# Moving the shared expert's down products and the overflow tables of a mixture-of-experts stage from the first pair of units to a place behind the seventh pair

## What is computed

```python
N_EXPERTS = 64
TOP_K = 8
D_EXPERT = 256
def moe(h, lp):
...
    def block(args):
        tb, gb = args
        a = jax.nn.silu(jnp.einsum('td,edf->tef', tb, lp['w_exp_gate'])) * jnp.einsum('td,edf->tef', tb, lp['w_exp_up'])
        a = a * gb[:, :, None].astype(a.dtype)
        return jnp.einsum('tef,efd->td', a, lp['w_exp_down'])
...
    shared = (jax.nn.silu(t @ lp['w_sh_gate']) * (t @ lp['w_sh_up'])) @ lp['w_sh_down']
    return (routed + shared).reshape(b_, l_, d)
```

## Time and profile before

| | |
|---|---|
| median of 3 runs | 787.26 us |
| the profiled execution | 786.93 us |
| its span | 785.1 us |
| PE busy | 742.6 us (95%) |
| DVE, ACT, POOL busy | 383.4, 136.3, 42.9 us |
| moved by DMA | 268.72 MB, mean 342 GB/s |
| time outside the span | 1.83 us |

### The profile page before, as it was taken

The page is one execution under the profiler, slowest core; times in us unless marked ns, Lnnn a source line. Parts: engine busy times, 40 slices in busy tenths (PEclk is TensorE's granted clock), DMA queues, the critical chain, the costliest instruction groups (busy, mean ns, idle before and its releaser), DMA issues.

```text
span 785.1 us, 13758 instructions
## 1 busy us (share of the span) xinstructions
PE 742.6 (95%) x5059; PEld 357.3 (46%) x5059; DVE 383.4 (49%) x869; ACT 136.3 (17%) x290; POOL 42.9 (5%) x49
## 2 busy tenths in 40 slices
PE   4999999889999999999999999899999999999988
PEld 0554434566555454544444444344444443444433
DVE  2236368483786334454454354344543454435456
ACT  3124001410111121111111111111110111111110
POOL 0000001000000110110100101101001011010100
PEclk9999999999999999999999999999999999999999
DMA  9993465650818969999999999999999999999992
GB/s 342 386 386 141 172 237 233 243 175 21 312 33 349 355 241 383 399 420 419 418 419 421 418 422 418 418 421 418 421 419 419 421 417 421 419 419 421 419 389 84
DMA packets 52218, 268.72 MB, mean 342 GB/s; under 512 B 6556, under 2 KB 8988, under 8 KB 27104
## 3 DMA queue, kind: packets, MB, share of 16 engines
q1 hardware_dynamic: 47584, 255.78, 81.0%
q0 software_dynamic: 4608, 12.59, 4.2%
HBM read 269.01 MB, written 3.52 MB: 347 GB/s over the span
## 4 chain that ended last, share of the span: by engine, by line
PE 59%; DMA 31%; DVE 5%; SPq 2%; issue 2%; ACT 1%; DVEq 0%; ACTq 0%
PE ps L555 55%; DMA raw_gu<-in_w_exp_up 29%; PE ps L1011 1%; DMA ada<-in_w_ada 1%; SPq L484 1%; SPq L485 0%; PE ps L866 0%; DVE probT L1624 0%; DVE x L1698 0%; PE ps L1038 0%; DVE xtmp L1696 0%; PE ps L632 0%; DVE h L1722 0%; DVE keyT L1569 0%; DVE h L1723 0%
## 5 line engine op out<-in xcount | busy, mean ns | idle before, releaser
L555 PE MATMUL ps<-raw_gu,xs 128*32 128x512 f32 x2048 | 226.1, 593 | 18.1 <-DMA raw_gu<-in_w_exp_up 16.7
L555 PEld LDWEIGHTS ps<-raw_gu,xs 128*32 128x32 f32 x2048 | 68.9, 110 | 172.5 <-issue 157.6
L555 PE MATMUL ps<-raw_dn,ast 128*32 128x512 f32 x824 | 116.3, 595 | 0.1
L1971 DVE TENSOR_TENSOR acc<-acc,ps 128x512 f32<-128x512 f32 x180 | 109.9, 678 | 0.0
L1928 DVE SCALAR_TENSOR_TENSOR act_a<-ps,small,sil 128x256 f32<-128x256 f32 x32 | 15.5, 484 | 192.1 <-ACT sil L1334 192.1
L555 PE MATMUL ps<-ys,place 128*128 128x512 f32 x360 | 98.4, 409 | 0.0
L555 PEld LDWEIGHTS ps<-ys,place 128*128 128x128 f32 x360 | 63.3, 189 | 35.7 <-issue 25.1
L1964 DVE TENSOR_TENSOR ys<-ps,ys 128x512 fp32r<-128x512 f32 x60 | 41.5, 691 | 66.0 <-ACT ys L1347 66.0
L555 PEld LDWEIGHTS ps<-raw_dn,ast 128*32 128x32 f32 x824 | 28.8, 109 | 60.4 <-issue 58.2
L1347 ACT CAST ys<-ps 128x512 fp32r<-128x512 f32 x60 | 35.1, 585 | 111.7 <-PE ps L555 111.7
L2080 POOL DMA_INDIRECT xg<-h_spill,slot_row x30 | 29.7, 988 | 435.5 <-DVE slot_row L1882 430.9
(11 more groups left out here) (319 smaller groups left out, 692.3 us busy)
## 6 DMA issues: line engine op xcount, KB each, us to landing
raw_gu<-in_w_exp_gate SPq DMA_DIRECT2D x64, 1024.0 KB, 16.0
raw_gu<-in_w_exp_up SPq DMA_DIRECT2D x64, 1024.0 KB, 18.1
raw_dn<-in_w_exp_down SPq DMA_DIRECT2D x48, 1024.0 KB, 16.8
ada<-in_w_ada SPq DMA_DIRECT2D x16, 512.0 KB, 11.3
ada2a<-in_w_ada SPq DMA_DIRECT2D x8, 1024.0 KB, 4.6
ada2b<-in_w_ada SPq DMA_DIRECT2D x8, 1024.0 KB, 6.2
raw_dn11a<-in_w_exp_down SPq DMA_DIRECT2D x16, 512.0 KB, 17.3
raw_dn11b<-in_w_exp_down SPq DMA_DIRECT2D x16, 512.0 KB, 21.1
```

Of the source, the lines that this page charges most:

```text
L555: return nc.tensor.matmul(out, l, r, start=first, stop=last)
L1971: V.tensor_tensor(a, a, ps[:, 4 + (6 * half + k) % 4, :], ALU.add).then_inc(S["acc_done"], 1)
```

## The change

The three `shared_down` and `over_tables` leave pair 0 on PE and stand behind the loop over pairs 1 to 6, in PSUM banks of their own numbering (`rest`, banks 4 to 7), between `down(6, 1)` and `up(7, 0)`. `shared_turn` stays. ACT's six copies into `acc` go; DVE starts `acc` by copying the first scattered results instead of adding them, and behind pair 6 it makes the tables and adds the six shared results to `acc`. PE starts pair 7 when all nine results are taken. SP, ACT, DVE and POOL get a second loop each, so that the first (up to pair 6) needs no table; the read of `jobs` and the wait for `tables_ready` stand between the two. `sh_aT` moves to other addresses. The core of the diff:

```diff
+        rest = ["overR", "overJ", "overK"] + [f"sd{t}{n}" for t in range(NT) for n in range(2)]
+        SPLIT = WIDE // 2 + 1
+        def rbank(n):
+            return ps[:, 4 + rest_no[n] % 4, :]
...
-            sp.wait_ge(S["tables_ready"], 1)
-            n_pairs = sp.value_load(jobs[0:1, NJOB:NJOB + 1], min_val=NMAIN // 2, max_val=NUNIT // 2)
-            with sp.Fori(1, n_pairs - 1) as p:
+            with sp.Fori(1, SPLIT) as p:
+                next_weights(p)
+            sp.wait_ge(S["tables_ready"], 1)
+            n_pairs = sp.value_load(jobs[0:1, NJOB:NJOB + 1], min_val=NMAIN // 2, max_val=NUNIT // 2)
+            with sp.Fori(SPLIT, n_pairs - 1) as p:
+                next_weights(p)
...
+            def open_rest(n):
+                if rest_no[n] > 3:
+                    pe.wait_ge(S["rest_taken"], rest_no[n] - 3)
+                return rbank(n)
...
             shared_turn(2)
-            pe.wait_ge(S["hr_sb"], hr_no["sa2"] + 1)
-            shared_down(0)
             turn(0, 0, True)
-            over_tables()
-            shared_down(1)
             pe.wait_ge(S["misc_sb"], freed_all)
             pe.wait_ge(xg_in[1], 16)
             for n in range(2):
                 tokens_t(1, n)
-            shared_down(2)
             pe.wait_ge(S["pick_ready"], 2)
             pe.wait_ge(S["ast_ready"], 2)
             gate_slots(2)
             pe.wait_ge(S["hr_sb"], len(hr))
             down(0, 0, False)
...
-            with pe.Fori(1, WIDE // 2 + 1) as p:
+            with pe.Fori(1, SPLIT) as p:
                 pair(p, True)
-            with pe.Fori(WIDE // 2 + 1, final) as p:
+            pe.wait_ge(S["xs_act"], 2 * SPLIT + 2)
+            pe.wait_ge(S["xs_dve"], 2 * SPLIT + 2)
+            over_tables()
+            for t in range(NT):
+                shared_down(t)
+            pe.wait_ge(S["tables_ready"], 1)
+            n_pairs = pe.value_load(jobs[0:1, NJOB:NJOB + 1], min_val=NMAIN // 2, max_val=NUNIT // 2)
+            final = pe.value_load(jobs[0:1, NJOB + 1:NJOB + 2], min_val=NMAIN // 2 - 1, max_val=NUNIT // 2 - 1)
+            pe.wait_ge(S["rest_taken"], len(rest))
+            with pe.Fori(SPLIT, final) as p:
                 pair(p, False)
...
-            shared_out(0)
             take_turned(0, 0)
-            shared_out(1)
             tokens(0, 1)
-            shared_out(2)
...
-            add_scattered(0, 1)
+            for k in range(6):
+                dve.wait_ge(S["scat_done"], 6 + k + 1)
+                V.tensor_copy(acc[:, k // 2, k % 2 * 512:(k % 2 + 1) * 512], ps[:, 4 + (6 + k) % 4, :]).then_inc(S["acc_done"], 1)
...
+            with dve.Fori(1, SPLIT) as p:
+                pair(p)
+            i = take_rest("overR")
...
+            dve.sem_inc(S["tables_ready"], 1)
+            dve.wait_ge(S["acc_done"], 12 * SPLIT)
+            for t in range(NT):
+                for n in range(2):
+                    a = acc[:, t, n * 512:(n + 1) * 512]
+                    taken(V.tensor_tensor(a, a, take_rest(f"sd{t}{n}"), ALU.add))
...
+            with pool.Fori(0, SPLIT) as p:
+                pool.wait_ge(S["xt_done"], 4 * p + 4)
+                gather(p + 1)
             pool.wait_ge(S["tables_ready"], 1)
```

More of the change, by code:

```diff
@@ L270, in build @@
         sh_a = [at(f"sh_a{t}", 58 + t, [P, DE]) for t in range(NT)]
-        sh_aT = [at(f"sh_aT{t}", 74 + t, [P, 2, P]) for t in range(NT)]
+        sh_aT = [at(f"sh_aT{t}", (201, 202, 123)[t], [P, 2, P]) for t in range(NT)]
         acc = at("acc", 34, [P, NT, D])
@@ L363, in build @@
                 + ["A20", "A21", "pv2", "mT10", "mT11", "o2", "mT20", "mT21"]
-                + ["pos", "key", "tabR", "tabP", "tabG", "tabJ", "tabK", "start", "overR", "overJ", "overK"])
+                + ["pos", "key", "tabR", "tabP", "tabG", "tabJ", "tabK", "start"])
         misc_no = {n: k for k, n in enumerate(misc)}
@@ L377, in build @@
         hr = [f"{n}{t}{x}" for t in range(NT) for n, x in (("h", 0), ("h", 1), ("r", ""))] \
-            + [f"sa{t}" for t in range(NT)] + [f"sd{t}{n}" for t in range(NT) for n in range(2)]
+            + [f"sa{t}" for t in range(NT)]
         hr_no = {n: k for k, n in enumerate(hr)}
@@ L391, in hbank @@
         def hbank(n, w=512):
-            if n[0:2] == "sd":
-                return ps[:, 1 + int(n[3]), 0:w]
             return ps[:, hr_no[n] % 2, 0:w]
         combos = [(0, 0), (1, 0), (0, 1), (1, 2)]
+        rest = ["overR", "overJ", "overK"] + [f"sd{t}{n}" for t in range(NT) for n in range(2)]
+        rest_no = {n: k for k, n in enumerate(rest)}
+        SPLIT = WIDE // 2 + 1
+        def rbank(n):
+            return ps[:, 4 + rest_no[n] % 4, :]
         last_order = [(n, t) for n in range(2) for t in (1, 2, 0)]
@@ L999, in over_tables @@
                     last = mm(w, ones[0:NE], offs[0:NE].unsqueeze(2).to_broadcast([NE, NOVER, 2]), False, True)
-                last.then_inc(S["misc_done"], 1)
-                o = open_misc("overK")
+                last.then_inc(S["rest_done"], 1)
+                o = open_rest("overK")
                 for t in range(NT):
@@ L1304, in shared_turned @@
                 nc.scalar.copy(sh_aT[t][:].rearrange("p f j -> p (f j)"), hbank(f"sa{t}", 2 * P)).then_inc(S["hr_sb"], 1)
[L1306 to L1310, removed]
             norm2(0)
@@ L1370, in _, with pair @@
             high_y(0, 1)
[L1371 to L1375, removed]
+            def pair(p):
                 silu(p, 0)
@@ L1384, in _ @@
                 high_y(p, 1)
+            with act.Fori(1, SPLIT) as p:
+                pair(p)
+            act.wait_ge(S["tables_ready"], 1)
+            n_pairs = act.value_load(jobs[0:1, NJOB:NJOB + 1], min_val=NMAIN // 2, max_val=NUNIT // 2)
+            final = act.value_load(jobs[0:1, NJOB + 1:NJOB + 2], min_val=NMAIN // 2 - 1, max_val=NUNIT // 2 - 1)
+            with act.Fori(SPLIT, final) as p:
+                pair(p)
             with act.Fori(final, n_pairs) as p:
@@ L1938, in _ @@
             gated(0, 0)
[L1940 to L1957, removed]
             def low_y(p, half):
@@ L2013, in residual, with pair @@
                 V.tensor_tensor(x1[:, t], x1[:, t], acc[:, t], ALU.add).then_inc(S["z_ready"], 1)
-            with dve.Fori(1, final) as p:
+            def pair(p):
                 dve.wait_ge(S["gates_done"], p + 1)
@@ L2030, in _, with take_rest, taken @@
                 low_y(p, 1)
+            with dve.Fori(1, SPLIT) as p:
+                pair(p)
+            def take_rest(n):
+                dve.wait_ge(S["rest_done"], rest_no[n] + 1)
+                return rbank(n)
+            def taken(i):
+                i.then_inc(S["rest_taken"], 1)
+            i = take_rest("overR")
+            own(V.tensor_copy(jobs[0:1, NE:NJOB], i[0:1, 0:NOVER]))
+            taken(V.tensor_scalar(pcmp[0:1], lc("four")[0:1], i[0:1, NOVER:NOVER + 1], None, ALU.is_lt))
+            dve.wait_ge(S["rest_taken"], 1)
+            own(V.tensor_reduce(pcount[0:1], pcmp[0:1], AX.X, ALU.add))
+            own(V.tensor_scalar(jobs[0:1, NJOB:NJOB + 1], pcount[0:1], float(NMAIN // 2), None, ALU.add))
+            own(V.tensor_scalar(jobs[0:1, NJOB + 1:NJOB + 2], pcount[0:1], float(NMAIN // 2 - 1), None, ALU.add))
+            i = take_rest("overJ")
+            V.memset(posq[:, :, QMAIN + QOVER:], -1.0)
+            taken(V.scalar_tensor_tensor(posq[:, :, QMAIN:QMAIN + QOVER], i[:, 0:NT * QOVER].rearrange("p (t j) -> p t j", t=NT), -1.0,
+                                         off[:, :, QMAIN:].to_broadcast([P, NT, QOVER]), ALU.add, ALU.subtract))
+            V.memset(gmov[:, :, NUNIT:, :].bitcast(F32), 0.0)
+            taken(gates(take_rest("overK"), NMAIN, NUNIT))
+            dve.wait_ge(S["rest_taken"], 3)
+            dve.sem_inc(S["tables_ready"], 1)
[4 more added lines that the diff above has]
+                    taken(V.tensor_tensor(a, a, take_rest(f"sd{t}{n}"), ALU.add))
+            n_pairs = dve.value_load(jobs[0:1, NJOB:NJOB + 1], min_val=NMAIN // 2, max_val=NUNIT // 2)
+            final = dve.value_load(jobs[0:1, NJOB + 1:NJOB + 2], min_val=NMAIN // 2 - 1, max_val=NUNIT // 2 - 1)
+            with dve.Fori(SPLIT, final) as p:
+                pair(p)
             with dve.Fori(final, n_pairs) as p:
```

26 lines of the change are left out of this document (11 added, 15 removed).

## The result

| | before | after |
|---|---|---|
| median of 10 runs | 788.58 us (786.84 to 790.26) | 783.05 us (782.46 to 790.0) |
| the profiled execution, its span | 786.93, 785.1 us | 783.13, 781.3 us |
| start of `up(0, 0)` | 266.32 us | 267.54 us |
| from there to the end of the span | 518.8 us | 513.8 us |

The ratio of the times is 0.994, with an interval of 0.9924 to 0.9956: 5.5 us or 0.6% faster. The forecast was 777.4, with a range up to 781.0; the time lies outside. The rest of the document looks for those.

A forecast was written before the change was run, and what follows sets the result against it. The prediction took the DMA stream of weights, once it runs without a gap, to bound the kernel. 786.93 - 10.6 + 0.8 = 777.1 us against the profiled execution, 777.4 for the median; range 775.0 to 781.0.

The forecast's parts named there:

- The bound: Whole kernel: the end is the moment DMA began to stream without a gap, plus the bytes left.
- `down(0, 0)` 12.1 us earlier: Pair 0 on PE: with the moved work gone, `down(0, 0)` starts at 277.1 instead of 289.24.
- Term 1: Pair 0: DMA no longer stands still or runs slowly from 285 to 330 us; -10.6 us, bound -10.9.
- The margin of 1.9 us at unit 4: Tightest weight issue after pair 0: the queue lasts 1.9 us past the time the new issue flows.
- D: Seam behind pair 6: time the moved work takes there on PE; 13.9 us, bounds 13.0 and 14.9.
- PE's slack as a cover: Behind the seam: PE's 14.8 us of waits for weights hide the 13.9 us, with 0.9 to spare.
- Term 2: Seam behind pair 6: issue for unit 16 13.3 us late, queue covers 12.5, DMA stands still; +0.8 us.
- Rival 1: Seam: an engine stalls 4.5 us, exceeding the covers; 781.9 us; chance 0.09.
- Rival 2: Pair 0: gather or a table holds `down(0, 0)` by 4 us, opening a 2.1 us gap; 779.5; chance 0.08.
- Rival 3: Seam: PE frees no weight buffer, queue nearly empty, DMA stands still for the full 13.3 us; 791.3; chance 0.04.
- What was to show it wrong: DMA hole over 2 us behind the seam, `down(0, 0)` after 279, or no PE weight waits after the seam and late end.

The follow-up runs named there:

- the kernels without a dent: Changed kernel with less or divided work at the seam, so the stream shows no dent; 507.8 us from `up(0, 0)` to the end.
- one tile: Against the changed kernel: shared down products of token tiles 1 and 2 and their additions left out at the seam; 777.62 us, ratio 0.9854.
- two portions: Against the changed kernel: tables and tile 0 behind pair 6, tiles 1 and 2 behind pair 10; 777.6 us, once more 778.3.

## Why the prediction was wrong, step by step

*The bound: right.* The end is where the stream stopped standing still, plus the bytes. Every kernel's loss shows as dents in the stream that are within 1 us of it.

*`down(0, 0)` 12.1 us earlier: right.* It starts 9.99 us after `up(0, 0)`, before 22.92 (289.24 - 266.32), so 12.9 earlier.

*Term 1, -10.6 us: right.* 518.8 - 507.8 = 11.0 by the kernels without a dent; that is just beyond the bound of -10.9, which from its rows comes to -10.8. The margin of 1.9 us at unit 4 held: 418 GB/s from 292 to 330.

*D = 13.9 us: right*, 14.1. The last addition and its semaphores hold PE 1.17 us, forecast 0.9.

*PE's slack as a cover: right that it suffices, wrong that it is used up.* I expected the waits behind the seam to shrink to 1 or 2 us and they are 7.3. 14.8 less the 8.1 that the queue covered would be 6.7; the other 6.0 of PE's absence delayed DMA as much, and PE waits for it again. The first wait came at unit 9 (0.33 us, then 1.49 at unit 10), not at unit 12: PE gained more in pair 0 than DMA, so it catches up with the stream sooner. The prediction told this the wrong way round ("the stream catches up with it"): from 330 to 450 us it is PE that comes nearer to the stream, since it needs 30.0 us a pair where the stream needs 31.9. The chain of before:

```profile
335.02 12.04 PE ps L555 x102
...
364.98 12.04 PE ps L555 x102
```

*Term 2, +0.8 us: the step that failed, 6.0 measured.* The prediction put it so: "At that moment the queue held unit 15's gate and up weights, landed at 507.62, and its down weights, 2.1 MB or 5.0 us more, to 512.6", less 1.4, a cover of 12.5 us for an issue that is 13.3 late, or 13.1 against D, which counts the wait of 0.62 too. Measured: 8.1. Five of those microseconds were not there. The step that failed is thus the size of this one term, how much work the queue held; that the queue covers was right. By trace the change is worth -11.0 + 6.0 = -5.0 us, where the forecast had -10.6 + 0.8. The bytes show most of the five. What the queue of the weights moved in before, from 507.6 us to the end:

```profile
q1 hardware_dynamic: 16011, 102.85, 89.6%
```

Had nothing of unit 15's down weights moved when its gate and up weights landed, 2.10 of these, 16 units of 6.29 MB and 1.57 of output would have been left, 104.33 MB. 102.85 were. The trace of after confirms the count: from 503 us on, when the queue was empty, it moved just the 16 units and the output, 102.24 MB:

```profile
q1 hardware_dynamic: 15840, 102.24, 88.9%
```

So 1.48 of the 2.10 MB had moved already: 1.48 MB at 0.419 MB a us are 3.5 us that I counted twice. When a load counts as landed, a good part of the next one has thus moved. The Trainium skill, page "DMA: Bandwidth & Descriptors", section "Why a DMA increments its semaphore by 16 and not by 1", says that the up to 16 engines of a transfer finish independently and the semaphore counts them; the bytes agree, with 1.48 MB ahead. They do not tell how much of this is that spread and how much is the time from a load's last byte to PE's start. At the other end the rate falls in steps too: in after 385, 313 and 66 GB/s over 6 us instead of a sudden stop. The remaining 1.5 us may lie there and in the restart; no run separates them, and their cause stays open. Some 0.8 of them stand in the dent of 5.3 us, 0.7 outside it.

*The rivals.* Rival 1 (a stall at the new code) did not come: PE's idle time of 1.17 us is put down to DVE, and one tile with the same loops loses 0.1 us. It gave 781.9, near the time measured, but by a mechanism that is not there. Rival 2 did not come. Rival 3 had the mechanism: DMA idle behind the seam because no buffer is freed. I gave it 0.04 because I let it decide only for a cover under 4.1 us, as all or nothing. A cover of 8.1 against D lies between the 13.1 of the forecast and the 3.3 that its 4.1 comes to in the same terms (4.1 counts the 1.4 of the start, and not the wait of 0.62). It gives just this time: 777.4 + (13.1 - 8.1) = 782.4, and 783.7 against the median of the ten runs (783.05 measured). The range should have carried the cover as an unknown of several us; I had bounds for D, on which less hung, and none for the queue.

*What was to show it wrong* did: a hole of more than 2 us behind the seam.

## What to carry to other kernels

Before a long piece of work is put between two stages of a streaming loop, ask how long the engine that frees the buffers may be away: count the bytes that are left in the queue at that moment from bytes moved, not from when a load landed, since here 3.5 us of the next load had moved by then. Work longer than that is cut into portions, each no longer than the cover, with enough rounds between for the lead to come back; here two portions gave twice the gain of one. And a gain at the front can be measured apart from its price further back by varying the length of the moved work alone.

## What the runs showed of the hardware that was not expected

*The clock at a short idle time.* With only the tables at the seam, PE does small products and then stands for 3.49 us, and the next product runs slowly:

```profile
484.05 0.51 DVE L1880 TENSOR_TENSOR gmov<-ps,gmov 128x336 fp32r<-128x336 f32 x1
486.64 9.97 PE L566 MATMUL ps<-raw_gu,xs 128*32 128x512 f32 x64 [3.49 <-issue]
```

```profile
L1158 PEldq TENSOR_LOAD <-jobs x1: 499/499/499, 484.7 to 484.7; - x1
L1159 PEldq TENSOR_LOAD <-jobs x1: 328/328/328, 485.6 to 485.6; - x1
```

```profile
484.00:488.00 4.00, 1.36 (x8) 0.46 (x12) 1.48 (x3) 0.00 (x0) 0.00 (x0) 0.71 1.01 422
488.00:492.00 4.00, 4.00 (x24) 1.15 (x20) 0.00 (x0) 0.00 (x0) 0.00 (x0) 0.50 1.02 418
```

Only the first 1.4 us are a wait for DVE's last table, done at 484.56. In the other 2.1 PE's sequencer reads `jobs` twice, from 484.7 to 485.9, and goes on to the next loop, with no product left to run beside it. In the change the same reads begin at 488.8, beside the shared products, and cost nothing, as the prediction had it. The granted clock is 0.71 and then 0.50, which is 1.2 GHz, and `up(14)` takes 9.97 us instead of 7.07. With the shared products between tables and `up(14)` the clock stays at 1.00. The 2.9 us come on top of its D of 5.9: 8.8 against a cover of 8.1 gives 0.7, and the loss was 0.9. The tables left in pair 0 brought the clock to 0.50 with a wait of only 1.15 us, after small products. In these two kernels small products and a wait cost more than their own length, by what ran slowly behind them; 1.17 us of waiting behind the 24 large products of the change did not lower the clock.

*A lead of the stream has no sharp end.* DMA falls over some 6 us from 426 GB/s to 2, and comes back within about two: from 504 to 506 it moved 225 GB/s, as much as if it had flowed at 419 from 504.9 on, 1.6 us after the issue at 503.35.
